# Dot products of gathered expert rows that read the tile's tokens from PSUM

## What is computed

```
def second_block(x, ...):
    for layer in range(DEPTH_2):
        h = rmsnorm(x, norm_mix[layer]) * (1.0 + sc1) + sh1
        y = even_mixer(h, ...) if layer % 2 == 0 else odd_mixer(h, ...)
        x = x + g1 * y
        h = rmsnorm(x, norm_ffn[layer]) * (1.0 + sc2) + sh2
        x = x + g2 * peer_ffn(h, peer_w_q[layer], peer_sub_keys[layer], peer_u[layer], peer_v[layer])
    return rmsnorm(x, norm_final)

def peer_ffn(h, w_q, sub_keys, u, v):
    ...
    def chunk(args):
        xc, ec, gc = args                 # 128 tokens, their 128 experts, their gates
        act = jax.nn.gelu(jnp.einsum('cd,ced->ce', xc, u[ec]))
        return jnp.einsum('ce,ced->cd', gc.astype(xc.dtype) * act, v[ec])
```

## Time and profile before

| | |
|---|---|
| median of 3 runs | 2596.34 us (2588.57 to 2601.74) |
| the profiled execution | 2572.51 us, span of its instructions 2570.8 us |
| busy: PE, DVE, POOL, ACT | 1748.5, 1607.1, 1210.6, 368.3 us |
| mean granted TensorE clock | 0.82 of full speed |
| DMA | 757.92 MB, of which 587.27 MB from POOL's queue |

### The profile page before, as it was taken

How to read it: one execution, slowest core, us unless ns; L and a number is a source line. 1 busy time by engine, 2 the same in 40 slices (tenths; PEclk the granted TensorE clock), 3 DMA queues, 4 the chain that set the end, 5 groups by cost and what they waited for, 6 DMA issues and landing times.

```text
span 2570.8 us, 23368 instructions
## 1 busy us (share of the span) xinstructions
PE 1748.5 (68%) x7234; PEld 1206.3 (47%) x7234; DVE 1607.1 (63%) x3441; ACT 368.3 (14%) x977; POOL 1210.6 (47%) x1124
## 2 busy tenths in 40 slices
PE   7999699998987245764657657645776745255555
PEld 5887587886866223532245336325544522011112
DVE  3348515602143997599774855997495698766764
ACT  1012501101021021110111211011131101000001
POOL 1001001100000367477775674777577577877773
PEclk9899899999987668887788778878887887667767
DMA  8556447953424679999999899999989999899995
GB/s 290 193 163 225 136 139 268 361 155 107 131 82 131 212 264 370 358 373 372 356 384 409 293 377 364 384 343 370 406 296 372 366 340 359 318 384 362 382 364 231
DMA packets 210157, 757.92 MB, mean 295 GB/s; under 512 B 23036, under 2 KB 26248, under 8 KB 209800
## 3 DMA queue, kind: packets, MB, share of 16 engines
q0 software_dynamic: 161280, 587.27, 61.3%
q1 hardware_dynamic: 48344, 167.35, 18.7%
q10 hardware_dynamic: 432, 2.03, 0.2%
HBM read 755.50 MB, written 1.07 MB: 294 GB/s over the span
## 4 chain that ended last, share of the span: by engine, by line
PE 37%; DVE 21%; POOL 20%; issue 14%; DMA 4%; ACT 2%; another core or an unknown queue 2%; DVEq 0%; SPq 0%; ACTq 0%
PE psL L423 32%; POOL W L414 20%; DVE W L908 5%; DVE Z L843 3%; DMA W<-experts_v,crow 2%; PE psO L423 2%; PE psS L423 2%; DMA wring<-weights 2%; DVE N L843 1%; DVE bias L1313 1%; DVE bias L1325 1%; DVE bias L1316 1%; DVE Z L849 1%; DVE N L846 1%
## 5 line engine op out<-in xcount | busy, mean ns | idle before, releaser
L423 PE MATMUL psL<-W,con 128*128 128x512 f32 x1024 | 630.8, 765 | 452.9 <-ACT con L1432 235.2
L414 POOL DMA_INDIRECT W<-experts_u,crow x512 | 593.4, 1159 | 605.4 <-DVE crow L846 357.8
L908 DVE SCALAR_TENSOR_TENSOR W<-W,Z 128x1024 f32<-128x1024 f32 x512 | 612.6, 1223 | 178.3 <-DMA W<-experts_u,crow 147.0
L423 PE MATMUL psL<-N,wring 128*128 128x256 f32 (+1 forms) x3568 | 630.2, 338 | 95.5 <-DVE N L846 52.3
L414 POOL DMA_INDIRECT W<-experts_v,crow x512 | 566.1, 1106 | 267.2 <-issue 157.3
L423 PEld LDWEIGHTS psL<-N,wring 128*128 128x128 f32 x3568 | 563.2, 200 | 168.6 <-DVE N L846 55.1
L423 PEld LDWEIGHTS psL<-W,con 128*128 128x128 f32 x1024 | 229.9, 241 | 811.9 <-issue 591.7
L843 DVE SCALAR_TENSOR_TENSOR Z<-W,crow,Z 128x1024 f32<-128x1024 f32 x252 | 324.0, 1286 | 57.6 <-DMA W<-experts_v,crow 50.9
L398 POOL DMA_DIRECT2D W<-ada x96 | 50.9, 530 | 453.1 <-DVE W L1038 452.3
L1432 ACT ACTIVATE Z<-psL 128x128 f32<-128x128 f32 (+2 forms) x190 | 60.0, 319 | 624.4 <-PE psL L423 527.4
L1432 ACT ACTIVATE con<-con,crow 128x128 f32<-128x128 f32 x256 | 86.4, 391 | 412.3 <-DVE crow L849 285.5
(11 more groups left out here) (197 smaller groups left out, 1303.1 us busy)
## 6 DMA issues: line engine op xcount, KB each, us to landing
wring<-weights SPq DMA_DIRECT2D x311, 512.0 KB
W<-ada POOLq DMA_DIRECT2D x96, 512.0 KB, 5.7
W<-experts_u,crow POOLq DMA_INDIRECT x512
W<-experts_v,crow POOLq DMA_INDIRECT x512
W<-rel_rows SPq DMA_DIRECT2D x1, 1536.0 KB, 9.0
X<-x_dram ACTq DMA_DIRECT2D x1, 1024.0 KB, 5.8
out<-N SPq DMA_DIRECT2D x1, 1024.0 KB, 3.9
W<-rel_rows SPq DMA_DIRECT2D x1, 768.0 KB, 5.0
```

The source lines that it names most:

```text
L414: pool.indirect_dma_start(W[:, slot * D:(slot + 1) * D], None, experts_u if kind == "u" else experts_v, bass.IndirectOffsetOnAxis(ap=idx[: ...
L423: return pe.matmul(o, l, r, start=first, stop=last)
L908: dve.scalar_tensor_tensor(out=row, in0=row, scalar=1.0, in1=h_t[T], op0=ALU.mult, op1=ALU.mult, accum_out=dots[:, col:col + 1]).then_inc( ...
```

## The change

The tile's tokens are copied once by ACT, when the tile's stream begins, into `psL` 0 and 1, called `hps`. The u dots read them there instead of from SBUF. The first u dot of a tile waits for this copy (`h_held`). To free the two banks, `project_beside` takes turns between `psO` and `psT` (with a wait for the last transpose's reader before the first unit in `psT`), the sums of the norms of one tile go to `psS` 0, and the attentions of `even1`, `odd0` and `odd1` (`LATE`) hold their two score maps once, in `psS` 0 and 1, not for two jobs in turn; a job's scores wait until the job before it has been read.

```diff
+        hps = psL[:, 0:2, :].rearrange("p b n -> p (b n)")
+        beside = (psO, psT)
+        LATE = ("even1", "odd0", "odd1")
...
+        def score(kind, n, m, w):
+            return psS[:, m, 0:w] if kind in LATE else (psL if m else psS)[:, n % 2, 0:w]
...
                     pe.wait_ge(out_taken, OUT0[name] + j - 1)
+                    if j == 1 and turns[0]:
+                        pe.wait_ge(turn_taken, turns[0])
                     for k in range(KC):
-                        m = mm(psL[:, j % 2, 0:P], w[:, k * P:(k + 1) * P], rhs(k), k == 0, k == KC - 1)
+                        m = mm(beside[j % 2][:, 0:P], w[:, k * P:(k + 1) * P], rhs(k), k == 0, k == KC - 1)
...
-                    m = mm(psO[:, 0:S if T is None else P], C("mean", P),
+                    m = mm(psO[:, 0:S] if T is None else psS[:, 0, 0:P], C("mean", P),
...
                     n, T = jb["n"], jb["T"]
-                    if n >= 2:
+                    if kind in LATE:
+                        pe.wait_ge(smax_ready, n)
+                    elif n >= 2:
                         pe.wait_ge(smax_ready, n - 1)
...
-                        o = (psL if m else psS)[:, n % 2, 0:w]
+                        o = score(kind, n, m, w)
...
                         if kind == "u":
-                            dve.scalar_tensor_tensor(out=row, in0=row, scalar=1.0, in1=h_t[T], op0=ALU.mult, op1=ALU.mult,
+                            if i == 0:
+                                dve.wait_ge(h_held, t + 1)
+                            dve.scalar_tensor_tensor(out=row, in0=row, scalar=1.0, in1=hps, op0=ALU.mult, op1=ALU.mult,
                                                      accum_out=dots[:, col:col + 1]).then_inc(row_dve, 1)
...
-                        f(query(l, T, half * 8 + j), psL[:, j % 2, 0:P], ACT.Copy).then_inc(out_taken, 1)
+                        f(query(l, T, half * 8 + j), beside[j % 2][:, 0:P], ACT.Copy).then_inc(out_taken, 1)
...
                 rows(NROUND)
                 begin(l * NT + T)
+                act.wait_ge(turn_taken, turns[0])
+                for b in range(2):
+                    m = f(hps[:, b * 512:(b + 1) * 512], h_t[T][:, b * 512:(b + 1) * 512], ACT.Copy)
+                m.then_inc(h_held, 1)
```

More of the change, by code:

```diff
@@ L254, in build @@
         diag_ready, acc_taken = sem("diag_ready"), sem("acc_taken")
+        h_held = sem("h_held")
         stored = sem("stored")
@@ L286, in rounds @@
                 body(m % per, m // per)
-        def ring_of(name):
-            return 2 if UNIT0[name] >= UNIT0["eout0"] else 4
+        def score(kind, n, m, w):
+            return psS[:, m, 0:w] if kind in LATE else (psL if m else psS)[:, n % 2, 0:w]
         def spread(n, j, of):
@@ L425, in _ @@
             stream = {"tile": None}
+            turns = [0]
             def begin(t):
@@ L456, in project @@
                     pe.wait_ge(out_taken, OUT0[name])
-                ring = ring_of(name)
                 def unit(j, i):
@@ L462, in unit @@
                     if not (isinstance(i, int) and OUT0[name] + i * 8 + j < 4):
-                        pe.wait_ge(out_taken, OUT0[name] + i * 8 + j - ring + 1)
+                        pe.wait_ge(out_taken, OUT0[name] + i * 8 + j - 3)
                     for k in range(KC):
-                        m = mm(psL[:, j % ring, 0:cols], w[:, k * P:(k + 1) * P], rhs(k), k == 0, k == KC - 1)
+                        m = mm(psL[:, j % 4, 0:cols], w[:, k * P:(k + 1) * P], rhs(k), k == 0, k == KC - 1)
                     m.then_inc(unit_done, 1)
@@ L569, in attention @@
                     rows(1)
-            turns = [0]
             def turn(pairs, tile=psT):
@@ L937, in residual @@
                     dve.wait_ge(unit_done, UNIT0[name] + o + 1)
-                    p = psL[:, o % ring_of(name), 0:S if T is None else P]
+                    p = psL[:, o % 4, 0:S] if T is None else beside[o % 2][:, 0:P]
                     x = chunk(X, o) if T is None else toks(X, o, T)
@@ L953, in norm @@
                 dve.wait_ge(ss_ready, n + 1)
-                link(ts(var[:, 0:w], psO[:, 0:w], EPS, None, ALU.add))
+                link(ts(var[:, 0:w], psO[:, 0:w] if T is None else psS[:, 0, 0:w], EPS, None, ALU.add))
                 dve.reciprocal(var[:, 0:w], var[:, 0:w]).then_inc(rv_ready, 1)
@@ L976, in front @@
                     for m in range(2):
-                        ins = stt(Sb[:, b, m * S:m * S + w], (psL if m else psS)[:, b, 0:w], 0.125, jb["bias"][m],
+                        ins = stt(Sb[:, b, m * S:m * S + w], score(kind, n, m, w), 0.125, jb["bias"][m],
                                   ALU.mult, ALU.add)
@@ L1641, in odd @@
                     act.wait_ge(unit_done, UNIT0[f"oin{T}"] + j + 1)
-                    f(toks(Z, j, T), psL[:, j % 2, 0:P], ACT.Copy).then_inc(out_taken, 1)
+                    f(toks(Z, j, T), beside[j % 2][:, 0:P], ACT.Copy).then_inc(out_taken, 1)
                     rows(spread(6, j, 25))
```

## The result

The changed kernel takes 2613.15 us (median of 20 runs, 2592.58 to 2622.45), the kernel before 2597.49 (20 runs): a ratio of 1.0048, 95% interval 1.0029 to 1.0068. It is a little slower; the forecast was 2540 and a gain of 56. The profiled execution has a span of 2590.9 us against 2570.8.

The account below looks back on a forecast made before the run. The prediction took POOL's row issues, stretched by u dots, to set the pace in several stretches, under DMA's 410 GB/s. Gains of 61 us less 5 of costs, net 56, took 2596.3 to 2540 us; range 2505 to 2585.

Parts of the forecast that it names:

- u dots, duration: The 512 u dots on DVE take no longer with tokens in PSUM: 0 us each, bounds 0.06 us either way.
- rival E: A dot whose second input comes out of two PSUM banks takes longer, kernel slower, 2633 us; 5%.
- What stretches an issue: POOL's issues wait only for DVE operations with two SBUF inputs; 197 us over, some five sixths from u dots.
- Rival D: Dots with PSUM second still hold up POOL's issues; only the costs are left, 2601 us; 6%.
- Scores once, projections, copy: Costs around the dots: scores held once 4.5 us, projections 0, copy into hps 0.5.
- rival B: Freed issues fall into v sums, waiting 0.6 us one row in four; gain 10 to 30, 2576 us; 17%.
- the term of 2220 to 2535: Last tile's rows: v sums still in the way, at best 25 us gained, 10 us taken.
- Mostly near their ends, 0.09: v sums meet POOL's issues mostly near the sums' ends, lengthening an issue by 0.09 us instead of 0.6.
- the fourth: POOL's pace sets the kernel's in 1235 to 1290, most of 1420 to 1525, and 2220 to 2535.
- the forecast's 15, 16, 8 and 22 us for the four tiles: Gains from u dots no longer holding up POOL's issues, put by tile; their sum is 61 us.
- this sign: What would refute the forecast: POOL's busy time falls and the span doesn't; then its pace wasn't the kernel's.
- the forecast's 30 to 80: Gain in us in the forecast's own case, u dots no longer holding up issues, 2515 to 2566 us; 60%.

Follow-up runs that it names:

- a2_no_lock: Changed kernel with the v sums too reading one input from PSUM, v rows on DVE not summed up: 1.0159 and 1.0181 of the kernel before.
- a1: Changed kernel with the u dots reading the tokens from SBUF again, all else kept: 1.0024 and 1.0023 of the kernel before.
- session 3: A later stretch of measuring on one chip, with its own runs of the kernel before (2497.5 us); no unit late in any of four traces.
- a0_again: The changed kernel itself, unedited, measured again: 0.9818 of the kernel before.
- b5_pause: Kernel before with three waits on semaphores long reached ahead of each issue, which made no pause: 1.0007 of the kernel before.
- b10: Kernel before with only the last tile's u dots and v sums in PSUM: 0.9972 and, repeated, 0.9948 of the kernel before.
- a8_paced: Changed kernel with POOL clearing 16 numbers per partition and waiting for that ahead of each issue: 1.0152 of the kernel before.

## Why the prediction was wrong, point by point

**u dots, duration.** Forecast 0; measured 1218 ns against 1223. Right, and rival E falls. The surcharge for a PSUM source that the Trainium skill's page "VectorE: DVE Perf Modes" gives (The TRN2 errata) doesn't show for this form either.

**What stretches an issue** (third). Right: a2_no_lock has 5 us over in place of 197. Rival D falls. The Trainium skill, "SBUF — State Buffer" (Who interferes with whom), says that a GpSimd instruction that reads SBUF contends with two-input operations; the runs agree. It also infers that descriptor generation doesn't; the runs show otherwise for these indirect issues, 5 us over against 197.

**Scores once, projections, copy.** Forecast 5 us; a1 measured 5 to 6, twice. Right as a sum; no run tells the three apart.

**The v sums in the dots' place** (rival B, and the term of 2220 to 2535). An issue that begins within a v sum, over 0.1 us before its end, took 1.07 us on average before and takes 1.44 now; their excess over 0.94 grew from 24 to 102 us. "Mostly near their ends, 0.09" didn't survive the change. B named it and was half right: POOL's total fell by 93, where it would have fallen by some 170 with the v sums as before. It isn't what decided: without any of it, a2 is slower still.

**The step that failed is the fourth**, "where POOL's pace is the kernel's pace", with every term that hangs on it: the forecast's 15, 16, 8 and 22 us for the four tiles came out as 1, -11, -18 and 6. I read windows in which POOL is full and took for granted that the slots and the other engines would keep up with a faster POOL. In the first session they don't, since TensorE's signals come late: the waits behind late units grew by 43 us and POOL's late slots by 26. The two overlap in part, so they are a measure of size and no sum; by the medians the change is 16 us slower here and 41 faster without late signals, 57 us apart. In 2220 to 2535 POOL's busy time fell from 238 to 225 with as many issues, and its idle time grew by as much (315 - 225 - 68 = 22 us, 9 before). The forecast had named this sign: POOL's busy time falls and the span doesn't.

**How good the sum is without late signals.** In session 3, a0_again against b5_pause, tile by tile from POOL's first issue to its last: 412 to 404, 424 to 409, 425 to 419, 356 to 332, gains of 8, 14, 6 and 24 us. The forecast's terms, summed over the same tiles: 15, 16, 8 and 22. The medians give 41 us less, where the net was 56 (b5_pause's trace stands 13 us above its median, so the gains by tile are rather too large). So the mechanism is right there, 41 us lies within the forecast's 30 to 80, and the sign is wrong in the other sessions, by a condition that the trace of before showed in "remote" waits and in 2% of its chain. A rival "TensorE's signals, already late by 117 us where DMA is full, take back what is fed faster" should have stood in the list, with a price of up to the whole gain.

## What to carry to other kernels

Before costing a faster feed, read what frees the feeder's slots, and how far each wait's end lies behind the end of the work that it waits for. In this case "remote" waits in a program on one core went with late signals: they stand in every trace with 36 or more late units and in none of session 3. A stage can be at their mercy while another engine looks full. Where a gain depends on such a condition, take it first in the stretch with the fewest handshakes, as b10 does; even there late rows took back 36 us. And measure in more than one session: the same edit was worth -1.8% in one and +0.5 to +0.8% in two others.

## What the hardware showed that I had not expected

- TensorE's completions reached ACT, DVE, SP and POOL late in five of six sessions. The longest wait was 25 us (a8_paced), 18 in the changed kernel. DVE's signals to POOL came in time meanwhile but for 3 issues, 5 us together. In these traces records of semaphores are missing as well (`row_pe` 200 for 256 increments, none missing in session 3). Three of SyncE's register instructions, 0.04 us otherwise, took 0.70 us each at 1348 to 1352 in the changed kernel. The cause stays open.
- Three indirect rows of 0.52 MB under way give 285 GB/s, four 331; without a cap 356 to 389.
- Three waits on semaphores long reached cost nothing within the 0.30 us between two issues; clearing 16 numbers and waiting for it added 0.09.
